# Down projections: a third unit of the second columns by seven products (a second one in the narrow FFNs)

## The reference, cut to what matters

```python
def swiglu(x, w_in, w_out):
    gate, up = jnp.split(x @ w_in, 2, axis=-1)
    return (jax.nn.silu(gate) * up) @ w_out
...
x = layer_norm(alpha * x + 0.5 * swiglu(x, w_ff1_in[l], w_ff1_out[l]), ln1_g[l], ln1_b[l])
...
x = x + swiglu_2(rms_norm(x, norm_ffn[i]), ffn_gate[i], ffn_up[i], ffn_down[i])
```

## Time and profile before

| | |
|---|---|
| median of three runs | 2283.67 us |
| profiled execution, its time | 2283.28 us |
| its span, first to last instruction | 2281.5 us |
| TensorE matmuls busy | 2248.5 us |
| VectorE busy | 1623.9 us |
| ScalarE busy | 1192.6 us |

### The profile page before, as it was taken

One profiled execution on the slowest core, in us unless ns is written; L12 is line 12 of the kernel. 1 busy time (PEld: TensorE's weight loads), 2 busy tenths in 40 slices (PEclk: granted clock), 3 DMA queues, 4 the chain that ended last, 5 costly groups with the idle time before them and its releaser, 6 DMA issues.

```text
span 2281.5 us, 34563 instructions
## 1 busy us (share of the span) xinstructions
PE 2248.5 (99%) x14127; PEld 1928.4 (85%) x14127; DVE 1623.9 (71%) x2491; ACT 1192.6 (52%) x1872; POOL 129.0 (6%) x185
## 2 busy tenths in 40 slices
PE   8999999999999999999999999999999999989999
PEld 7888899888888888888898887888878888867887
DVE  5777768857777777768668667776877778666776
ACT  5555446534555545555356444655444555546553
POOL 2100010120000000000100110000000000420000
PEclk9999999999999999999999999999999999999999
DMA  6765564435565556656564436665645666643654
GB/s 225 225 192 190 188 223 121 140 121 179 191 190 191 182 193 203 190 192 197 190 184 139 128 116 208 199 192 174 212 162 166 205 192 195 196 126 110 196 181 148
DMA packets 283568, 408.17 MB, mean 179 GB/s; under 512 B 13701, under 2 KB 170689, under 8 KB 283153
## 3 DMA queue, kind: packets, MB, share of 16 engines
q1 hardware_dynamic: 275600, 380.91, 52.2%
q0 software_dynamic: 7808, 25.04, 3.7%
HBM read 403.98 MB, written 1.91 MB: 178 GB/s over the span
## 4 chain that ended last, share of the span: by engine, by line
PE 88%; DVE 7%; ACT 3%; issue 1%; DMA 1%; SPq 0%; DVEq 0%; ACTq 0%
PE PS L558 24%; PE PS L464 12%; PE PS L466 12%; PE PS L465 12%; PE PS L557 11%; PE PS L461 2%; PE PS L462 2%; PE PS L463 2%; DVE WL L1362 2%; PE PS L560 2%; PE PS L481 1%; PE PS L541 1%; PE PS L540 1%; PE PS L539 1%; DVE QX L1657 1%
## 5 line engine op out<-in xcount | busy, mean ns | idle before, releaser
L1362 DVE TENSOR_TENSOR WL<-RW,WH 128x1024 fp32r<-128x1024 f32 x682 | 808.9, 1219 | 174.9 <-ACT WH L981 171.1
L558 PE MATMUL PS<-XT,WH 128*128 128x512 f32 x2368 | 808.1, 395 | 0.0
L981 ACT ACTIVATE WH<-RW 128x1024 fp32r<-128x1024 f32 x682 | 685.4, 1042 | 233.8 <-PE PS L466 63.1
L557 PE MATMUL PS<-XT,WL 128*128 128x256 f32 x2072 | 581.5, 281 | 0.0
L558 PEld LDWEIGHTS PS<-XT,WH 128*128 128x128 f32 x2368 | 425.8, 188 | 75.5
L557 PEld LDWEIGHTS PS<-XT,WL 128*128 128x128 f32 x2072 | 390.3, 188 | 13.4
L464 PE MATMUL PS<-WH,XT 128*128 128x512 f32 (+4 forms) x640 | 249.4, 390 | 3.9 <-DVE WL L1362 2.9
L466 PE MATMUL PS<-WH,XT 128*128 128x512 f32 (+4 forms) x640 | 240.6, 376 | 0.0
L465 PE MATMUL PS<-WL,XT 128*128 128x512 f32 (+4 forms) x640 | 240.2, 375 | 0.0
L464 PE MATMUL PS<-WH,HTH 128*128 128x512 f32 x488 | 192.6, 395 | 0.0
L466 PE MATMUL PS<-WH,HTL 128*128 128x512 f32 x488 | 191.9, 393 | 0.0
(11 more groups left out here) (500 smaller groups left out, 3224.2 us busy)
## 6 DMA issues: line engine op xcount, KB each, us to landing
RW<-in_w_ff_in SPq DMA_DIRECT2D x256, 512.0 KB, 4.4
RW<-in_w_ff_out SPq DMA_DIRECT2D x128, 512.0 KB, 4.4
RW<-in_w_in SPq DMA_DIRECT2D x56, 512.0 KB, 4.7
RW<-in_w_gate SPq DMA_DIRECT2D x48, 512.0 KB, 4.3
RW<-in_ffn_gate SPq DMA_DIRECT2D x44, 512.0 KB, 4.5
RW<-in_ffn_up SPq DMA_DIRECT2D x44, 512.0 KB, 4.5
RW<-in_ffn_down SPq DMA_DIRECT2D x44, 512.0 KB, 4.6
RW<-in_w_out SPq DMA_DIRECT2D x16, 512.0 KB, 5.0
```

Source lines behind the costliest of these rows:

```text
L557: self.e.matmul(k.PS[:, b.n, 0:T], wl, k.XTH[:, kt, :], start=False, stop=False)
L558: ins = self.e.matmul(k.PS[:, b.n, :], wh, k.XT[:, kt, :], start=kt == 0, stop=kt == 7)
L981: self.e.activation(u.hi_out, raw, ACT.Copy).then_inc(*self.s["hi"].up(u.n))
L1362: self.e.tensor_tensor(u.lo_out, raw, u.hi_out.bitcast(F), ALU.subtract).then_inc(*self.s["lo"].up(u.n))
```

## The change

The second number for each width rises by one. In the second columns, the four wide down projections make the row pairs 8, 12 and now 16 by seven products, the two narrow ones 6 and now 10. The pair's tile HS becomes three blocks wide. The first columns stay as they are. By `down`, the order of the units of the second columns changes with the count, and so does the number of plain ones between.

```diff
 SEVEN = {32: (8, 12, 16, 20), 22: (6, 10, 14)}
-SEVEN_N = {32: (4, 2), 22: (3, 1)}
+SEVEN_N = {32: (4, 3), 22: (3, 2)}
```

## The result

Over 20 runs each the changed kernel takes 2288.24 us in the median (2282.8 to 2291.07) and the kernel before 2283.52 us; the ratio is 1.0017, 95% interval 1.0010 to 1.0023. That is 2.3 to 5.3 us slower. Forecast were 2284.7 us and a range up to 2287.2 us: the direction of the sum was right, its size was too small by about 3.5 us, and the median lies outside the range.

The account below looks back on a forecast made before the run. TensorE's matmuls were taken to bound the down projections if VectorE delivers in time. Terms -0.6 (w1 to w3), -0.3 (w4), +2.2 (n1), -0.3 (n2) sum to +1.0 us on 2283.67, median 2284.7 us; range 2281.9 to 2287.2.

Parts of the forecast that it names:

- TensorE's saving, 0.31 us for each, 1.86 in all: Six down projections: a seven-product unit (2.46 us) replaces 12 plain matmuls (2.77 us), 0.31 us less each, 1.86 in all.
- w1 to n2: Down projections by time: w1 to w4 of the FFNs of width 4096, n1 and n2 of those of width 2816.
- The cover inside the second columns: Second columns: VectorE's 2.65 us of added work per unit fits its 12 and 7.5 us unused, without TensorE waiting.
- w4, -0.3: Fourth wide down projection: the chain ends before the late group's first pass, so no delay; -0.3 us.
- E: End of the last unit by seven products in a down projection's second columns; chain times are counted from it.
- w1 to w3, -0.2 each: First three wide down projections: 0.31 us saved less 0.1 us of TensorE wait, -0.2 us each, -0.6 together.
- E + 14.7: First three wide down projections: chain's end with a 5.0 us third load, making the residual up to 0.7 us late.
- the choice between the bounds: First three wide down projections: TensorE wait of 0 to 0.4 us, taken as 0.1 for less traffic beside the load.
- n1, +2.2: First narrow down projection: residual 2.2 us late, no cover ahead of the transposes; +2.2 us, own saving included.
- The rule for the length of a load: Weight loads: 2.0 us plus bytes over 436 GB/s, 3.2 us, giving a sum about -1; the prediction used trace rows.
- The terms' upper bounds: Whole kernel: 3 x 0.1 - 0.3 + 2.5 - 0.3 = +2.2 us, up to one more if a cut meets traffic.
- Rival (c): Load-cut chain bites in all four wide down projections as in the first narrow, 2.2 us each; +10.7, 2294.4 us; chance 0.05.

Follow-up runs that it names:

- e6: Changed kernel with its counts kept but the second columns' seven-product units placed further ahead of the late group; ratio 0.9995 (0.9986 to 1.0004) against the kernel before.
- e2: Kernel before with the third seven-product unit in only the four wide down projections; ratio 1.0008 (0.9999 to 1.0017).
- e1: The kernel before, unchanged, timed against itself as yardstick; ratio 1.0004 (0.9995 to 1.0012).
- e8: Changed kernel with five raw buffers rather than four; 2275.99 us, ratio 0.9966 (0.9954 to 0.9979) against the kernel before.
- e9: Kernel before with five raw buffers rather than four; ratio 0.9979 (0.9970 to 0.9988).

## Why the prediction was wrong, point by point

**TensorE's saving, 0.31 us for each, 1.86 in all: too large; this is one step that failed.** What a down projection saved is its difference of length less the wait that it got: 0.17, 0.07, 0.14, 0.20, 0.25 and 0.19 us for w1 to n2, the same to 0.02 us in all three traces, 1.0 us in sum. The prediction took one unit by seven products (2.46 us) and one stretch of 12 matmuls (2.77 us) for all of them. Summed over the units by seven products of a down projection, one more of them cost 2.49 to 2.55 us: it comes with weights in an XT slot, and such units took 2.49 to 2.51 us in w1 before already (three of its six), a row that the prediction did not use. One plain unit less gave 2.65 to 2.77 us. Why it gave less in some, and w2 saves the least, was not followed up.

**The cover inside the second columns: right.** In none of the three traces does TensorE wait for a weight split there. e6, with all of the added weight work and the old distance, has no added wait in the wide ones.

**w4, -0.3: -0.15 to -0.24 us, right with some luck.** The chain was to end at E + 13.3, 0.6 us ahead of the first pass. It ended at E + 14.2, 14.1 and 14.2, just as the residual was due, because the load took 5.5 to 5.7 us and not the 4.8 us read in n1. The trace of before has this load in w4, with 6.2 us; the prediction did not use it. That a slightly longer wait there can bring 3 us at 1.2 GHz (e2) was not foreseen.

**w1 to w3, -0.2 each: the step that failed by most.** The chain was named, with its links in the right order, and its upper bound, E + 14.7, was what the first trace showed (residual at E + 14.6 in w1). The step that failed was the choice between the bounds: "I take 0.1 because the load ahead of this run is gone early, so that it has less traffic beside it". Its reason does not hold: in w1 before the change the load ahead of the run is gone too (at E + 1.1, four us ahead of the run), and the third load takes 5.0 us all the same; after the change it is gone at E + 1.2 to 2.4. The third load took 5.0, 5.8 and 5.7 us in the three traces of w1 and 5.2 to 5.8 us in w2 and w3, at or above the 5.0 that was put down as its long end. Taken at 0.1 us each, the added waits were 0.42 to 1.27 us each; over the three they sum to 2.0, 3.0 and 3.3 us in the three traces, where 0.3 was put down. Predicted -0.6 in sum, saving included, measured +1.58, +2.57 and +2.88 us.

**n1, +2.2: right in kind, too large in size.** +1.34 to +1.41 us. E came at 1924.40 (1924.44 was put down), the combining at E + 0.7, the earlier of the two starts considered, and the last load took 4.5 us rather than 4.8. The residual started at 1937.35, 1.4 us later than before, not 2.2. This error, 0.8 us, hid part of the two others.

**The rule for the length of a load was no better.** By the Trainium skill ("DMA: Bandwidth & Descriptors", section "Anatomy of one DMA") a load would take 3.2 us, an estimate (its fit is for the software path), and the sum would be about -1; both are ruled out, since the four loads of the run in w1 took 3.4 to 6.0 us. (The 0.6 us given for n1 by that estimate are those of a load of 3.6 us; with 3.2 us it would be 0.2.) The Trainium skill's rule that VectorE is strict first-in first-out ("TensorE: Matmul & The Clock Gate", "Architectural detail: the array is 16x 32x32, not 1x 128x128") held where it was looked at: in n1 of e6 ScalarE's copy for the combining is done at 1921.60, and VectorE starts the combining only behind a cut, at 1922.43. ScalarE's timeline:

```profile
1921.21 0.39 ACT L1039 ACTIVATE QS<-PS 128x256 f32<-128x256 f32 x1
```

**Sum.** In the first trace the added waits of w1 to w3 came out 1.7 us above the prediction, the saving 0.8 us below it, and n1's added wait 0.9 us below it; in the other two traces the first of these is 2.7 and 3.0 us. The down projections of the three traces give +2.64, +3.55 and +3.83 us where +1.0 was forecast; the medians give +4.2 to +4.7 us in three series. What is left, some 1 us, is open. It is no more than what the kernel before shows against itself (e1, +1.0 us), and the interval of the result, +2.3 to +5.3 us, holds the down projections alone as well. The changed kernel's executions had a mean granted clock of 0.9966 and those of before 0.9970, and executions with a lower clock take longer in both kernels, 1.1 to 1.5 us for 0.001; from these figures comes an estimate of some 0.5 us. But e1, the kernel before, had 0.9967, and no run isolates the clock.

The range was too narrow at its upper end. The terms' upper bounds give +2.2 us and one more for traffic, 2286.9 us (2287.2 was written). They allowed +0.1 for each of the first three wide ones; measured were +0.25 to +1.12. They should have taken a load longer than the 5.0 and 5.1 us of one run of four, since w4 of the same trace shows 6.2 to 6.6 us for the second to the fourth.

Rival (c), the chain biting in the wide ones, was the right mechanism with too high a price: waits of 0.4 to 1.3 us, not 2.2.

## What to carry to other kernels

In a kernel bound by one engine, the in-order queue of the second one has deadlines of its own. Draw the chain to the next of them (here last product, combining, cut, load, cut, residual, norm, transposes), measure its length against the distance in units of the bounding engine, and treat each reordering as a change of that distance, above all one that a formula for even spreading makes in passing. When the slack is below half a microsecond, read the load at the place in question and take it at its longest. Of the three ways tried here, one more raw buffer relieved the chain best: it made this change a gain, and the kernel with both edits (e8) is 7.7 us faster than the one before, of which the buffer alone gives 4.2 (e9).

## What the runs showed of the hardware that was not expected

One load of 512 KB (w1, the third behind the last product), at the same place of the same program and third of four issued 1.13 us apart, took 5.0 us in one execution and 5.7 to 5.8 us in two others. In w4, 1.9 to 2.2 us from the matmul to the transposes left TensorE at 2.4 GHz in thirteen of the fourteen traces; in e2 2.46 us were followed by 3.4 us at 1.2 GHz.
